# Writing out the expert loops of a hybrid diffusion backbone on one core

## What is computed

```python
s1, i1 = lax.top_k(s[:, :, 0], PEER_TOPK)          # 16 of 128 keys
s2, i2 = lax.top_k(s[:, :, 1], PEER_TOPK)
sc, ic = lax.top_k(cand, PEER_TOPK)                # 16 of the 16 x 16 sums
e = (jnp.take_along_axis(i1, ic // PEER_TOPK, axis=-1) * PEER_NKEYS
     + jnp.take_along_axis(i2, ic % PEER_TOPK, axis=-1))
g = jax.nn.softmax(sc, axis=-1)
a = jax.nn.gelu(jnp.einsum('chkd,cd->chk', u_tab[e], hc), approximate=False)
return jnp.einsum('chk,chkd->cd', (g * a).astype(v_tab.dtype), v_tab[e])
```

## Time and profile before

| | |
|---|---|
| median of 3 runs | 5880.15 us (5877.74 to 5890.0) |
| the profiled execution | 5882.08 us, its span 5880.3 us |
| PE, matmul | 4560.4 us, 78% |
| PE, weight load | 2499.2 us, 43% |
| DVE | 3701.1 us, 63% |
| POOL | 1947.4 us, 33% |
| ACT | 1235.2 us, 21% |
| mean granted clock of PE | 0.890 |
| read from HBM | 1498.04 MB, 255 GB/s over the span |

### The profile page before, as it was taken

How to read it: one execution, slowest core, us unless ns; L and a number is a source line. 1 busy time by engine, 2 the same in 40 slices (tenths; PEclk the granted TensorE clock), 3 DMA queues, 4 the chain that set the end, 5 groups by cost and what they waited for, 6 DMA issues and landing times. The chain is left out here.

```text
span 5880.3 us, 55023 instructions
## 1 busy us (share of the span) xinstructions
PE 4560.4 (78%) x14456; PEld 2499.2 (43%) x14456; DVE 3701.1 (63%) x8357; ACT 1235.2 (21%) x2648; POOL 1947.4 (33%) x1532
## 2 busy tenths in 40 slices
PE   6899879887776777777777777988977777777776
PEld 3585358764222332323322325745853222322322
DVE  6613442235777877877877776344135777877877
ACT  5521022212111111111111134412222111111111
POOL 4021013212343443444444432211423334444443
PEclk8999889988889888888888888999978889888888
DMA  5011012116999999999999981111316999999998
GB/s 219 15 58 47 15 37 64 61 36 256 381 385 399 383 381 388 394 385 380 397 385 383 397 356 46 58 47 36 97 53 272 379 380 398 377 381 396 383 378 344
DMA packets 223040, 1503.39 MB, mean 256 GB/s; under 512 B 25284, under 2 KB 25668, under 8 KB 51852
## 3 DMA queue, kind: packets, MB, share of 16 engines
q0 software_dynamic: 184320, 1342.26, 56.4%
q1 hardware_dynamic: 38412, 157.98, 7.4%
HBM read 1498.04 MB, written 2.10 MB: 255 GB/s over the span
## 5 line engine op out<-in xcount | busy, mean ns | idle before, releaser
L1755 PE MATMUL psum<-arena 128*128 128x512 f32 x5120 | 2552.2, 656 | 957.0 <-DVE arena L1851 951.3
L1739 POOL DMA_INDIRECT arena<-in_uv,arena x1280 | 1419.9, 1109 | 2059.1 <-PE psum L1755 1718.4
L1755 PEld LDWEIGHTS psum<-arena 128*128 128x128 f32 x5120 | 1041.2, 210 | 2467.2 <-DVE arena L1851 1359.2
L1843 DVE SCALAR_TENSOR_TENSOR arena<-arena 128x1024 f32<-128x1024 f32 x1280 | 1554.1, 1219 | 249.5 <-issue 194.0
L953 PE MATMUL psum<-view_at,view_at 128*128 128x512 f32 (+1 forms) x4896 | 951.1, 357 | 18.5 <-issue 9.7
L953 PEld LDWEIGHTS psum<-view_at,view_at 128*128 128x128 f32 x4896 | 814.3, 190 | 152.0 <-issue 20.7
L1773 ACT ACTIVATE arena<-arena 128x1 f32<-128x1 f32 x1280 | 252.3, 202 | 2927.2 <-DVE arena L1843 2926.3
L262 POOL TENSOR_TENSOR view_at<-view_at,view_at 128x1024 fp32r<-128x1024 f32 (+1 forms) x184 | 397.1, 2168 | 1369.8 <-ACT view_at L296 1368.5
L1851 DVE TENSOR_SCALAR arena<-ident,arena 128x128 f32<-128x128 f32 x1280 | 450.8, 352 | 57.0 <-ACT arena L1773 48.8
L1488 DVE TENSOR_TENSOR view_at<-view_at,psum 128x768 f32<-128x768 f32 (+1 forms) x48 | 39.4, 820 | 372.9 <-PE psum L953 372.9
L1877 DVE TENSOR_TENSOR arena<-psum,arena 128x1024 f32<-128x1024 f32 x80 | 98.0, 1224 | 267.7 <-PE psum L1755 267.7
(11 more groups left out here) (185 smaller groups left out, 3549.2 us busy)
## 6 DMA issues: line engine op xcount, KB each, us to landing
view_at<-in_w_in SPq DMA_DIRECT2D x108, 512.0 KB, 3.5
view_at<-in_w_mod SPq DMA_DIRECT2D x48, 1024.0 KB, 11.6
arena<-in_uv,arena POOLq DMA_INDIRECT x1280, 9.2
view_at<-in_w_br SPq DMA_DIRECT2D x48, 256.0 KB, 2.6
arena<-in_dft SPq DMA_DIRECT2D x2, 4096.0 KB, 15.1
view_at<-in_w_out SPq DMA_DIRECT2D x16, 512.0 KB, 7.4
view_at<-in_wq SPq DMA_DIRECT2D x16, 512.0 KB, 3.5
arena<-in_x SPq DMA_DIRECT2D x1, 2048.0 KB
```

The source lines that it names most:

```text
L1739: nc.gpsimd.indirect_dma_start(out=slots[k % RING], out_offset=None, in_=table, in_offset=bass.IndirectOffsetOnAxis(ap=eidx[:, p, k:k + 1] ...
L1755: last = nc.tensor.matmul(c.bank(2 * p + h), diag[:, k % 4], slots[k % RING][:, D + h * 512:D + (h + 1) * 512], start=(k == 0), stop=(k == ...
L1843: nc.vector.scalar_tensor_tensor(out=junk[:, k % 2], in0=slots[k % RING][:, 0:D], scalar=1.0, in1=h2N[:, bass.ds(t, 1)].rearrange("p a n - ...
```

## The change

On all four engines of `phase_experts` both `Fori` loops become loops of Python. The program holds every selection's instructions one after another: 48 in the first stage and 32 in the second, in place of two. `t`, `i` and `n` are numbers when the program is made, so each threshold is a constant, and the four operands that were addressed through a register are addressed directly. The work, its order on each engine, the waits, the slots and the buffers are the same.

```diff
-            with pool.Fori(0, nt) as t:
-                with pool.Fori(0, PH // 2) as i:
+            for t in range(nt):
+                for i in range(PH // 2):
                     for p in range(2):
                         n = t * PH + i * 2 + p
...
-            with pe.Fori(0, nt) as t:
-                with pe.Fori(0, PH // 2) as i:
+            for t in range(nt):
+                for i in range(PH // 2):
                     for p in range(2):
                         n = t * PH + i * 2 + p
                         pe.wait_ge(psum_used, n + 1)
...
             softmax_exp(0, 0)
-            with act.Fori(0, nt) as t:
-                with act.Fori(0, PH // 2) as i:
+            for t in range(nt):
+                for i in range(PH // 2):
...
-                do(nc.vector.tensor_copy(sc, scores[:, bass.ds(n, 1)].rearrange("p a n -> p (a n)")))
+                do(nc.vector.tensor_copy(sc, scores[:, n]))
...
-                                               in1=h2N[:, bass.ds(t, 1)].rearrange("p a n -> p (a n)"), op0=ALU.mult,
+                                               in1=h2N[:, t], op0=ALU.mult,
...
-            with dve.Fori(0, nt) as t:
-                with dve.Fori(0, PH // 2) as i:
+            for t in range(nt):
+                for i in range(PH // 2):
...
-                                                gate2[:, bass.ds(t // NT_LAT, 1)].rearrange("p a n -> p (a n)"),
+                                                gate2[:, t // NT_LAT],
                                                 ALU.mult).then_inc(psum_used, 1)
                         dve.wait_ge(psum_used, n + 3)
-                        x = c.xs[:, bass.ds(t, 1)].rearrange("p a n -> p (a n)")
+                        x = c.xs[:, t]
```

## The result

The written-out kernel takes 5694.23 us (median of 4 runs, 5689.77 to 5706.07) against 5878.94 us before: ratio 0.9686, 95% interval 0.9666 to 0.9707, 185 us faster. The forecast was 5715 us. The profiled execution is the longest of the four, 5706.07 us with a span of 5704.2.

A forecast was written before the change was run, and what follows sets the result against it. Transfers were taken to bound the expert stages nearly everywhere. Removing DVE's 38 backward branches saves 165 us, all other terms 0: 5882.1 - 165 = 5717, and with the median 2 us below the profiled execution 5715 us; range 5662 to 5778.

The forecast's parts named there:

- The suspect: DVE's 194.0 us of "issue" waits at L1843, laid to its 38 backward branches in the two expert stages.
- Rival C: A branch costs only 59 to 74 ns; DVE's hole is a wait for a landing: 5877 us, chance 0.04.
- The reason: DVE fetches its loop body, 20 KB, anew after every backward branch, through DMA engines full of gathers.
- the idle time of the DMA engines: Expert stages: only idle DMA share can be filled, 4.1 and 4.7 us a pair, 165 us in all.
- rival A: DVE sets the pace in the expert stages and landings keep up: all 214 us go, 5666 us, chance 0.18.
- Rival B: Gathers lose rate, to 400 GB/s, undrained or delayed by fetches: 108 us saved, 5772 us, chance 0.11.
- Register arithmetic: Loop register operations on all four engines, DVE's 68 a pair of 40 ns, run beneath working instructions: 0.
- The wait at L1877: DVE's wait for PE at each selection's end stays at 3.4 us.
- PE's clock: With a shorter pause PE's granted clock could stay up in the expert stages; taken at 0.
- The fetches of straight code: Written-out code on the four engines takes as many bytes as the five packets now and stops no engine: 0.
- rival D: Engines stop to fetch straight code, two stops on DVE a pair: 198 us more, 6078 us, chance 0.05.
- The rest of the kernel: Everything outside the expert stages, some 2400 us, must stay as it is.

The follow-up runs named there:

- e1: Only DVE's two loops written out, those of POOL, PE and ACT kept, against the kernel before: 5695.86 us, ratio 0.9673.
- e3: Full change, but DVE keeps its outer loop over tiles with eight selections in its body, so 8 backward branches in place of 38: 5729.78 us.
- e5: Kernel before with all its loops, 64 empty semaphore increments put ahead of DVE's loop in layer 0: 5681.64 us, ratio 0.9657.
- e9: Written-out kernel with table rows of 4 KB in place of 8, u half alone, used by PE in place of v: 5653.65 us.
- e8: Written-out kernel with L1877 and L1882 of every selection moved behind the third dot of the next selection: 5683.73 us.
- e2: POOL, PE and ACT written out, DVE keeps its loops, against the kernel before: 5891.37 us, ratio 1.0015.
- e12: The full written-out change run once more, unaltered, in later rounds: 5695.13 us.
- e6: Kernel before with all its loops, 8 empty semaphore increments put ahead of DVE's loop in layer 0: 5955.44 us, ratio 1.0125.
- e4: Written-out kernel, but ACT keeps its loops and gets eight empty semaphore increments behind each gelu, a body of 333 instructions: 5690.56 us.
- e7: DVE, PE and POOL written out, ACT's loop with its 333-instruction body moved by 64 empty increments ahead of it: 5748.38 us.
- e10: Kernel before, with its loops, and table rows of 4 KB in place of 8: 5795.37 us.

## Why the prediction was right, and where it was off

**The suspect, right.** The 194 us of "issue" at L1843 were DVE's 38 backward branches: `e1` gives all of the gain and `e3` 4.4 us a branch. Rival C, a landing under another name, falls with `e5`, where the landings are the same and the hole is gone.

**The reason, half right.** Fetching after the branch was right: DVE goes on 1.9 us behind the start of the packet, in all 38 cases. Why the body has to be fetched at all, the prediction left out; it gave its 20 KB, as if the size were the reason. It is not: ACT's 333 instructions ran without a stall and with one, and DVE's 320 likewise, by their place alone. The five packets an iteration held the answer already: at 8 KB a packet, a body of 20 KB needs three if it is well placed. I took the five as they were and did not ask why there were not three. What the runs show is that the place decides: with 0 and 8 empty instructions ahead of the loop there are five packets in each of the 38 iterations and a stall of 5.3 to 6.1 us, with 64 there are none and 0.3 us. That the blocks are of 8 KB (the packets of `q14` have 8192 bytes), that four of them are held, and that one of the four is taken by the block fetched ahead, fits every run but is the author's inference; no run shows it directly.

**The size: 185 us where 165 were forecast.** The mis-sized term is the idle time of the DMA engines. I counted (1.01 - 0.92) x 45.8 = 4.1 us a pair, and 4.7 in the second stage, and took the rate in the busy rest as unchanged. But the earlier trace rows also say that the first selection moved 371 / 0.92 = 403 GB/s per unit of share and the second 414 / 1.01 = 410; in the 4 us from 2350 it is 248 / 0.75 = 331. So the rate per share was low there too, and that was lost as well. Counted in bytes, a pair at the 410 GB/s of after is 33.56 / 0.410 = 81.9 us, 4.7 and 5.3 us less than 86.6 and 87.2; times 23 and 15 that is 188 us, and the expert stages became 189 us shorter. The steps after average 41.0 us in the first stage and 40.9 in the second, where 41.25 was forecast. But the 410 was known only afterwards: with the 414 GB/s of the second selection, whose share of 1.01 the forecast took as its measure, the same sum gives 219 us. Counting idle share was too low by some 50 us and holding 1.01 too high by some 30, and the 20 us of error are what is left of the two. That the time came out so near is in part luck.

**Which bound, right by a little.** For the transfers speak the share of 1.00, waits for landings up from 49.9 to 109.7 us, steps 0.4 us above the 40.6 of `e9`, and `e8`, where 255 us of DVE's waits go and the time falls by 10. But the steps lie halfway between the 41.25 us forecast and the 40.6 of rival A, and the time is 21 us from the one and 28 from the other (A: 5666 us): DVE and PE alone would be nearly as slow. Rival B, a rate of 400 GB/s, did not come.

**Costed at nothing.** Register arithmetic: right (`e2`, `e3`). The wait at L1877: 267.7 us before and 261.9 after, right. PE's clock: the mean granted clock of the long stretch rose from 0.87 to 0.92, with PE's pauses of 10 us gone (10.02 us ahead of 2344.80 before, 9.7 to 10.6 us at the 38 branches; after, none between two selections is over 5.3 us). The clock is 0.50 from 2340 to 2349 before and 1.00 from 2350. In time it shows little: DVE's wait for PE at L1877 fell by 6 us in all. The fetches of straight code were not quite nothing: DVE does not stop for them (0.6 us of "issue" at L1843), so rival D was wrong, but the expert stages take 6 us more than in `e5`, where the loops stay and hardly any code is fetched. The rest of the kernel was to stay as it is: outside the expert stages the profiled execution takes 2432.5 us, the repeat `e12` 2423.3 and the kernel before 2419.4. These 4 to 13 us are in no term of the prediction, and their cause is open.

## What to carry to other kernels

An "issue" wait of an engine behind a backward branch was a fetch of code here: DVE went on 1.9 us after the start of the packet, in all 38 cases. Read such a wait against the packets of the instruction queue in one iteration. The loop in `e5` brings none once it runs and has no stall; the same loop before brings five in every iteration, and stalls. Writing the loop out cured it here, and so did a shift of the code by 64 instructions, by the author's count because the body of 320 then lies in three blocks. A shorter body of DVE was not tried; ACT's 77 and POOL's 102 instructions in the kernel before go on 0.2 us behind their branches. What the stall costs is read from the stage's real bound, in bytes at the rate that it can hold and not in idle share. If a kernel with a loop changes its time after an edit ahead of the loop, suspect the place of the body before the edit: 8 empty instructions cost 75 us here.

## What was not expected of the hardware

- The same loop of 320 instructions ran at 5682, 5880 and 5955 us, by its place alone: 64, 0 and 8 empty instructions ahead of it. The difference is a stall of 5.5 us at each of 38 branches, and with 9 instead of 17 instructions on record before the sequencer's next pause a second one of DVE of 2.0 us (at 2370.09 in `e6`).
- From a taken branch to the next record of the sequencer it is 0.2 to 0.3 us on DVE and ACT where the loop brings no packets (`e5`, `e4`); where it brings five an iteration, 5.0 to 6.1 us under full gathers (before, `e6`, `e7`) and 3.2 to 5.3 us with the DMA engines at a share of 0.6 (`e10`).
- The first three packets behind such a branch of DVE start 5.0 us apart under full gathers (median of the 38 in the kernel before), at 3.7, 8.7 and 13.7 us in the pair at 2336.2; in `e10`, at a share of 0.6, the first two are 2.4 us apart (2.4 to 3.4).
